# Three-layer block kernel on one core: later key blocks summed by VectorE, decays behind the last convolutions, mirror blocks of the inverse by transposes, and four moved steps

## The reference, cut to what matters

```python
proj = h @ w_in; z, xbc, dt = split(proj)             # layer 0
xbc = silu(causal_dwconv(xbc, conv_w, conv_b))        # 24 tiles of 128 channels, 4 taps
acs = cumsum(softplus(dt + dt_bias) * A)              # decays, 32 heads
y = rmsnorm_groups(ssd_scan(xs, bm, cm, acs) * silu(z)) @ w_out
modulation = silu(c) @ mod_w + mod_b                  # rows of the layers' shifts, scales and gates
```

## Time and profile before

| what | us |
|---|---|
| median of 3 runs | 2679.03 (2676.23 to 2679.85) |
| the profiled execution | 2680.78 |
| its span in the trace | 2679.0 |
| TensorE busy (13456 matmuls) | 2559.1 |
| VectorE busy | 1217.1 |
| ScalarE busy | 1061.5 |
| GpSimd busy | 972.0 |

### The profile page before, as it was taken

The page is one execution under the profiler, slowest core; times in us unless marked ns, Lnnn a source line. Parts: engine busy times, 40 slices in busy tenths (PEclk is TensorE's granted clock), DMA queues, the critical chain, the costliest instruction groups (busy, mean ns, idle before and its releaser), DMA issues.

```text
span 2679.0 us, 36867 instructions
## 1 busy us (share of the span) xinstructions
PE 2559.1 (96%) x13456; PEld 2081.0 (78%) x13456; DVE 1217.1 (45%) x2007; ACT 1061.5 (40%) x1658; POOL 972.0 (36%) x431
## 2 busy tenths in 40 slices
PE   4999989999999999999999998999899999999998
PEld 2777768877888866669888887788668888988887
DVE  6777766576545746655111127554112111531122
ACT  3466644322225246654222235713342223442232
POOL 1333334455554210013444443302214445344443
PEclk9999999999999999999999999999999999999999
DMA  6433334577653200011333331201103333133231
GB/s 256 154 107 117 103 126 142 173 234 230 215 185 121 99 24 25 17 40 60 99 99 105 94 100 58 78 10 40 55 16 95 108 112 111 63 95 101 94 110 55
DMA packets 74994, 276.55 MB, mean 103 GB/s; under 512 B 8144, under 2 KB 10576, under 8 KB 73456
## 3 DMA queue, kind: packets, MB, share of 16 engines
q1 hardware_dynamic: 56672, 201.66, 23.8%
q10 hardware_dynamic: 18192, 73.08, 7.9%
HBM read 272.54 MB, written 2.16 MB: 103 GB/s over the span
## 4 chain that ended last, share of the span: by engine, by line
PE 84%; DVE 7%; DMA 4%; issue 3%; ACT 2%; DVEq 0%; SPq 0%; POOL 0%; ACTq 0%; POOLq 0%
PE G L293 28%; PE STAT_G L293 27%; DMA mod_w<-in_modw 3%; PE B L306 2%; DVE mod_w L347 2%; PE B L580 2%; PE B L293 2%; PE B L1314 2%; PE NRM L1351 1%; PE B L2336 1%; PE B L2022 1%; DMA const<-in_const 1%; PE STAT_G L1332 1%; PE STAT_G L306 1%; PE G L306 1%
## 5 line engine op out<-in xcount | busy, mean ns | idle before, releaser
L278 POOL TENSOR_TENSOR w_lo<-raw,w_hi 128x1024 fp32r<-128x1024 f32 x375 | 933.1, 2499 | 1655.6 <-ACT w_hi L270 1650.8
L270 ACT ACTIVATE w_hi<-raw 128x1024 fp32r<-128x1024 f32 x375 | 386.7, 1052 | 311.9 <-PE STAT_G L293 127.8
L293 PE MATMUL G<-h_hi,w_hi 128*128 128x512 f32 x888 | 352.2, 397 | 1.0 <-DVE tn L978 0.8
L293 PE MATMUL STAT_G<-h_hi,w_hi 128*128 128x512 f32 x872 | 346.5, 397 | 6.4 <-POOL w_lo L278 2.0
L293 PE MATMUL G<-h_lo,w_hi 128*128 128x512 f32 x888 | 346.0, 390 | 0.0
L293 PE MATMUL G<-h_hi,w_lo 128*128 128x512 f32 x888 | 345.8, 389 | 0.0
L293 PE MATMUL STAT_G<-h_lo,w_hi 128*128 128x512 f32 x872 | 340.4, 390 | 0.0
L293 PE MATMUL STAT_G<-h_hi,w_lo 128*128 128x512 f32 x872 | 340.4, 390 | 0.0
L347 DVE SCALAR_TENSOR_TENSOR mod_w<-mod_w,const 128x1024 f32<-128x1024 f32 x96 | 189.8, 1993 | 65.4 <-DMA mod_w<-in_modw 65.3
L293 PEld LDWEIGHTS G<-h_hi,w_hi 128*128 128x128 f32 x888 | 166.9, 188 | 41.4 <-issue 7.4
L293 PEld LDWEIGHTS STAT_G<-h_hi,w_hi 128*128 128x128 f32 x872 | 164.4, 189 | 43.9 <-issue 7.1
(11 more groups left out here) (553 smaller groups left out, 4408.6 us busy)
## 6 DMA issues: line engine op xcount, KB each, us to landing
raw<-in_units SPq DMA_DIRECT2D x375, 512.0 KB, 3.6
mod_w<-in_modw ACTq DMA_DIRECT2D x96, 512.0 KB, 4.7
mod_first<-in_modw ACTq DMA_DIRECT2D x8, 1024.0 KB, 20.2
acsb<-acs ACTq DMA_DIRECT2D x16, 512.0 KB, 3.6
cw<-in_cw ACTq DMA_DIRECT2D x2, 2048.0 KB, 8.7
x<-in_x SPq DMA_DIRECT2D x1, 2048.0 KB, 26.8
out<-x SPq DMA_DIRECT2D x1, 1024.0 KB, 4.8
out<-x SPq DMA_DIRECT2D x2, 512.0 KB, 3.1
```

Of the source, the lines that this page charges most:

```text
L270: act.activation(w_hi[s][:, :], raw[s][:, :], ACT.Identity).then_inc(hi_done, 1)
L278: pool.tensor_tensor(w_lo[s][:, :], raw[s][:, :], w_hi[s][:, :].bitcast(F32), ALU.subtract).then_inc(lo_done, 1)
L293: ins = pe.matmul(out[0:m, :], a[s][:, k * P:k * P + m], b[:, c], start=(n == 0 and q == 0), stop=(n == len(blocks) - 1 and q == 2))
```

## The change

It has seven parts. (1) At the end (`post_ffn2`, no next layer) the first sums of the second half are issued in the middle of the last unit's half product. (2) At the five seams ScalarE's Ln and Exp for the second half (`late_root` of `_b`) come behind the first high part of the first half. (3) In the GDN convolutions the reciprocal and two small operations move behind convolution 6, the rest of `decays()` behind convolution 7, TensorE's turn to t = 9, VectorE's copies and the Exp to t = 10. (4) In the inverse the L1652 products go; four groups of four transposes of g_y follow each level's Y update, into the same PSUM banks, and ScalarE copies each bank to g_x. (5) In sb VectorE adds the later key blocks in pairs and threes (three adds of 128x128 per head), and TensorE does nine matmuls of 512, 384, 256 and 128 columns (triangular) and 128, 256, 128, 128 and 128 columns (-1). (6) In layer 0 the scale and scan of the decays, and the DMA of their result, move behind convolution 0. (7) The row sums move up: block 11 is loaded and summed behind convolution 7, 12 is loaded before the 16 tiles and summed before tile 8's norm, 13 before tile 12's, 14 before tile 14's, 15 behind tile 15's; ScalarE's loads of 13 to 15 stand behind output copies instead of before them.

```diff
@@ late_tensor
+                if j == 7 and not more:
+                    product_half(pe, u1 + j, hi, lo, 1, banks[1][3], range(n // 2), n)
+                    late_sums(pe, name, 1, y0, range(3))
+                    done = n // 2
                 product_half(pe, u1 + j, hi, lo, 1, banks[1][j - 4], range(done, n), n).then_inc(unit_done, 1)
...
-            late_sums(pe, name, 1, y0)
+            late_sums(pe, name, 1, y0, range(4) if more else range(3, 4))
@@ late_scalar
-            late_root(act, name + "_b", 1, h0 + POST_B, B6)
             for i in range(KC):
                 late_high(act, k0, i, 0, bcol)
+                if i == 0:
+                    late_root(act, name + "_b", 1, h0 + POST_B, B6)
@@ gdn_tensor
-                if t == 5:
+                if t == 9:
                     pe.wait_ge(gab, 9)
...
                     pe.wait_ge(inv_c, n + 1)
+                    if lv > 1:
+                        pe.wait_ge(inv_x, n - TT + 1)
                     for h in range(4):
                         ins = pe.matmul(packed(UB[c], lv, h * 64, 64), g_x[c][:, hb[h]], half(g_qs[c], lv, 1, h * P, P),
                                         start=True, stop=True)
-                    if lv < LEVELS - 1:
+                    ins.then_inc(inv_mm, 1)
+                if lv < LEVELS - 1:
+                    for c in range(TT):
+                        n = (lv - 1) * TT + c
+                        pe.wait_ge(inv_done, n + 1)
                         for h in range(4):
-                            ins = pe.matmul(packed(UB[c], lv, 256 + h * 64, 64), g_qs[c][:, hb[h]],
-                                            half(g_x[c], lv, 0, h * P, P), start=True, stop=True)
-                    ins.then_inc(inv_mm, 1)
+                            ins = pe.transpose(UB[c][:, hb[h]], g_y[c][:, hb[h]], ident)
+                        ins.then_inc(inv_t, 1)
@@ gdn_scalar
-                if t == 8:
+                if t == 10:
                     act.wait_ge(gab, 10)
...
+            for n in range((LEVELS - 2) * TT):
+                act.wait_ge(inv_t, n + 1)
+                act.activation(g_x[n % TT][:, :], UB[n % TT][:, :], ACT.Identity).then_inc(inv_x, 1)
@@ gdn_vector
-                if t == 1:
-                    decays()
                 if 4 <= t <= 11:
                     l2(t - 4)
+                if t == 6:
+                    beta()
                 if t == 7:
+                    decays()
+                if t == 10:
                     decay_columns()
@@ sb_tensor
-                        for j in range(i, 4):
-                            _, _, oj, wj = ZT[j]
-                            ins = pe.matmul(ZB[m % 2][b][:, c + (j - i) * P:c + w], cst("ntri" if i == j else "nones"),
-                                            s_sp[m % 2][:, oj:oj + wj], start=False, stop=(j == 3), skip_group_check=True)
+                        pe.matmul(ZB[m % 2][b][:, c:c + w], cst("ntri"), s_sp[m % 2][:, o:o + w], start=False,
+                                  stop=(i == 3), skip_group_check=True)
+                    pe.wait_ge(later_done, 3 * m + 3)
+                    for i, j, src in later_keys(m):
+                        b, c, o, w = ZT[i]
+                        ins = pe.matmul(ZB[m % 2][b][:, c + j * P:c + j * P + src.shape[1]], cst("nones"), src, start=False,
+                                        stop=(i == 2 or j == 2), skip_group_check=True)
@@ sb_vector
+                v.wait_ge(sp_done, n + 1)
+                v.tensor_tensor(of1, sp[:, o2 + P:o2 + 2 * P], sp[:, o3:o3 + P], ALU.add).then_inc(later_done, 1)
+                v.tensor_tensor(of0[:, 0:P], sp[:, o1 + P:o1 + 2 * P], sp[:, o2:o2 + P], ALU.add).then_inc(later_done, 1)
+                v.wait_ge(later_done, 3 * n + 2)
+                v.tensor_tensor(of0[:, P:2 * P], sp[:, o1 + 2 * P:o1 + 3 * P], of1, ALU.add).then_inc(later_done, 1)
@@ ssm_scalar
+                if t == 1:
+                    act.wait_ge(dt_v, 6)
+                    act.dma_start(dram["acs"], dts[:, 2 * T:3 * T]).then_inc(acs_out, 16)
-                if t in (2, 4):
+                if t in (2, 4, 6):
                     mod_load(act, 8 + t // 2)
...
-            mod_load(act, 11)
+            mod_load(act, 12)
...
             high(8)
-            mod_load(act, 12)
+            high(9)
             output(1)
             prep(act, u_out + 5)
-            high(9)
+            mod_load(act, 13)
...
             for o in (4, 5):
                 high(2 * o + 2)
                 high(2 * o + 3)
-                mod_load(act, 9 + o)
                 output(o)
                 prep(act, u_out + 4 + o)
+                mod_load(act, 10 + o)
             high(14)
             high(15)
-            mod_load(act, 15)
@@ ssm_vector
-            v.wait_ge(dt_v, 4)
-            v.tensor_scalar(dts[:, 0:T], dts[:, T:2 * T], nega[0:32, 1:2], None, ALU.mult).then_inc(dt_v, 1)
...
+                if t == 0:
+                    v.wait_ge(dt_v, 4)
+                    v.tensor_scalar(dts[:, 0:T], dts[:, T:2 * T], nega[0:32, 1:2], None, ALU.mult).then_inc(dt_v, 1)
+                    v.wait_ge(dt_v, 5)
+                    v.tensor_tensor_scan(dts[:, 2 * T:3 * T], const_row_ones, dts[:, 0:T], 0.0, ALU.mult,
+                                         ALU.add).then_inc(dt_v, 1)
-                if t in (1, 3, 5):
+                if t % 2:
                     mod_sum(v, 8 + t // 2)
...
-            mod_sum(v, 11)
             for o in range(4, KC):
+                if o != 5:
+                    mod_sum(v, 12 + (o - 4 if o == 4 else o - 5))
                 normal(2 * o)
                 normal(2 * o + 1)
-                mod_sum(v, 8 + o)
+            mod_sum(v, 15)
```

More of the change, by code:

```diff
@@ L539, in late_tensor, with late_sums @@
                 pre_sums(pe, name, 0, range(6, 8))
-            late_sums(pe, name, 1, y0)
-        def late_sums(pe, name, a, y0):
+            late_sums(pe, name, 1, y0, range(4) if more else range(3, 4))
+        def late_sums(pe, name, a, y0, parts=range(4)):
             p = posts[name]
@@ L547, in late_sums @@
             if a:
-                pe.wait_ge(yo_done, y0 + 6)
-                pe.matmul(out, onesf, diag[:, tokens[1]], start=True, stop=False)
-                for i in range(4):
+                if 0 in parts:
+                    pe.wait_ge(yo_done, y0 + 6)
+                    pe.matmul(out, onesf, diag[:, tokens[1]], start=True, stop=False)
+                for i in parts:
                     pe.wait_ge(ysq_done, 12 * p + 9 + i)
                     ins = pe.matmul(out, onesf, quarter(i), start=False, stop=(i == 3))
+                if 3 not in parts:
+                    return
             else:
@@ L1914, in gdn_vector @@
                     v.wait_ge(inv_mm, n + 1)
[L1915 to L1919 removed]
+                    ys = half(g_y[c], lv, 1)
+                    v.tensor_tensor(ys, ys, packed(UB[c], lv, 0, 256), ALU.subtract).then_inc(inv_done, 1)
             def values_out(c):
@@ L1975, in build, with later_sums, later_keys @@
         uS = at["sb"]
+        later_done = S("later_done")
+        def later_sums(m):
+            return sq[:, m % 2 * T:m % 2 * T + 2 * P], sq[:, m % 2 * T + 2 * P:m % 2 * T + 3 * P]
+        def later_keys(m):
+            sp, (of0, of1) = s_sp[m % 2], later_sums(m)
+            o1, o2, o3 = (ZT[i][2] for i in (1, 2, 3))
+            return ((0, 1, sp[:, o1:o1 + P]), (0, 2, of0), (1, 1, sp[:, o2:o2 + P]), (1, 2, of1), (2, 1, sp[:, o3:o3 + P]))
         def sb_tensor(pe):
@@ L2105, in sb_vector @@
                 ins.then_inc(sp_done, 1)
+                sp, (of0, of1) = s_sp[n % 2], later_sums(n)
+                o1, o2, o3 = (ZT[i][2] for i in (1, 2, 3))
+                v.wait_ge(sp_done, n + 1)
[3 more added lines that the diff above has]
+                v.tensor_tensor(of0[:, P:2 * P], sp[:, o1 + 2 * P:o1 + 3 * P], of1, ALU.add).then_inc(later_done, 1)
                 if n >= 4 and n % 2 == 0:
```

13 lines of the change are left out of this document (3 added, 10 removed).

## The result

| | before | after |
|---|---|---|
| median of the runs | 2679.44 (4 runs, 2676.23 to 2685.20) | 2639.44 (4 runs, 2633.95 to 2645.19) |
| the profiled execution | 2680.78 | 2640.55 |
| its span | 2679.0 | 2638.7 |

A forecast was written before the change was run, and what follows sets the result against it. TensorE, busy 96% of the span, was taken to bound the kernel. Terms -9.1, -5.8, -6.4, -5.1, -1.6, -1.3 and +1.2 made -28.1 from 2680.78, so 2652.7, given as 2651 with a range of 2641 to 2662.

The forecast's parts named there:

- More than the waits: Rival: output stage gains 4 more, sb 1.5, seams and start their upper bounds (3): 2643 us; chance 0.13.
- The lower clock behind that wait goes too: GDN convolutions: the half-rate stretch behind the 6.2 us wait for the Ln disappears, estimated at 1.4 us.
- sb's -5.8: sb: shorter sums save 0.91 us at five heads and 0.42 at three, adds covered: -5.8 us.
- Inverse: Inverse: transposes at 0.44 us replace 20 matmul groups at 0.893, all waits covered, full clock held: -9.1 us.
- End: Kernel's end: sums moved before the last product's end uncover VectorE's add and the Square: a loss of 1.2 us.
- The rival that the clock falls in the inverse: Rival: transposes end the full rate at each of five levels, costing 44 us more: 2695; chance 0.04.
- that a transpose costs what a matmul does: Rival, inverse: a transpose of this data is as dear as a matmul, 2660 us; chance 0.03.
- the convolutions: GDN convolutions: 6.2 us wait and 1.4 of lower clock go, 1.2 comes back: -6.4 us.
- the 1.2 of convolution 7: GDN convolutions: the moved reciprocal makes convolution 7 late, so TensorE waits 1.2 us.
- the output stage (-5.1): Layer 0's output stage: TensorE's waits of 3.7 and 1.4 us for output copies shrink to about nothing: -5.1.
- the seams (-1.3): Five seams: the wait before the first low-part product shrinks by 0.26 us each: -1.3.
- the start (-1.6): Start of layer 0: scale and scan leave the path before convolution 0, whose following product waited 1.80 us: -1.6.

The follow-up runs named there:

- e5: Parts 6 and 7 together on the kernel before: median 2666.78 against 2678.43, ratio 0.9956.
- e10: Parts 3, 4 and 5 on the kernel before: median 2658.59 against 2678.32, ratio 0.9930.
- e9: Part 2 alone on the kernel before: median 2672.95 against 2678.32, ratio 0.9980.
- e12: The kernel after with part 1 undone, timed: median 2637.15 us, where the whole change on the same chip had 2638.05.
- e11: The whole change again, unchanged: median 2638.05 against 2678.32 for the kernel before, ratio 0.9858.
- e1: The kernel before once more, unchanged: 2680.13 us.
- e4: The kernel after with part 1 undone, one execution: 2641.51 us.
- e3: Part 6 alone on the kernel before: 2678.47 us.
- e8: The kernel after without part 7, row blocks 11 to 15 loaded and summed where they were: 2641.93 us.
- e2: Part 7 alone on the kernel before: median 2669.35 against 2677.55, ratio 0.9974.
- e6: The kernel before with row sums of the reloaded buffer over 128 columns instead of 1024, loads kept: median 2670.77, ratio 0.9970.

## Why the prediction was off by its size

I go by my own steps. Taken alone the parts make -11.7 (6 and 7, e5), -19.7 (3 to 5, e10), -5.4 (2, e9) and +1.3 (1, e12), together -35.5 with an uncertainty of 3 to 5 on each of the first three, against -40.0 and -40.3 (e11) for the whole; mine made -28.1. The 4.5 between -35.5 and -40 are within these errors. My own bounds add up to -41.2, which covers the result; the range of 2641 to 2662 cut them short. In the rival *More than the waits*, the nearest to what came, seams and start at their upper bounds make 3.7 and not 3, so 2642; but it would have reached this number by waits, not by the clock.

*The step that failed: the lower clock behind waits.* The sum has it at one place only, "The lower clock behind that wait goes too ... my estimate 1.4", and puts it at nothing in the output stage, at the start and at the seams. A time can be split by the traces into work at the full clock, idle time of TensorE, and what the lower level costs, which is half of TensorE's busy time at that level. By these three my sum was -16.4, -10.3 and -1.4 (sb's -5.8 being 7.3 less work and 1.5 more waiting). The mean of before and e1 against the mean of after and e11 gives -16.2, -13.1 and -11.7. So the work was right to 0.2 (part of that is luck, since the long feed-forward stretch of before counts here as work), the waits were short by 3, and the clock by 10. What the lower level cost was 24.6 us in before, 34.5 in e1, 18.3 in after and 17.3 in e11.

*Right in mechanism and size.* Inverse: 8.85 us a level, no gap, -9.0; the 10 us that I leaned on for the clock held the transposes of rows 5 in their last 1 us only, so the full clock was settled by the runs of the change and not before. sb: -6.1, adds covered, wait of 1.8 at even heads. End: a loss of 1.28 (e4, e12) against 1.2. The rival that the clock falls in the inverse, and that a transpose costs what a matmul does, are both out.

*Right in size by luck: the convolutions.* -6.7 against my -6.4, with the 1.2 of convolution 7 where I had put it. But I had 5.0 less of waiting and 1.4 of lower clock; measured are 3.6 of waiting, since the first Ln is still 1.37 late, and 3.1 of clock. The fall behind the 6.2 held 2.88 us of busy time, so the 1.4 that I gave it is right; a second one, from 1649 to 1653, I hadn't looked for. Against the usual 145.0 us of this stretch e10 gains 7.7.

*Mis-sized: the output stage (-5.1).* "The two waits of TensorE for such copies are 3.7 and 1.4 ... -5.1" holds as far as waits go, but it is not the whole price. In six executions with the old order and whole sums (before, e1, e3, e8, e9, e10) the stretch took 118.2 to 120.3 us with 13.7 of idle time in the mean, in six with the new (after, e2, e4, e5, e11, e12) 108.7 to 110.7 with 7.5. So 6.1 are waits, against my 5.1, though not only the two I named; the lower clock cost 5.2 in the mean with the old order and 1.7 with the new, 3.5 that I had not priced. What moved in VectorE's queue are its waits for the loads: 12.7 to 17.9 us between convolution 0 and the seam with the old order, 1.6 to 3.7 with the new. This is the chain moved up one slot, which I had put at the far end of the bounds. Its row sums took 38.7 us in before and 42.4 in e1, 34.9 and 33.6 in after and e11. I had priced a sum at its duration in one row, 2.72, when it takes 1.22 alone and up to 3.4 beside a subtraction, but e2 (39.5) and e8 (36.1) show that the sums' length doesn't make the difference between the two orders.

*Mis-sized: the seams (-1.3) and the start (-1.6).* I priced the seams' wait, 0.26 each; it measured 0.25 to 0.33. Nothing behind a wait of 2 us was priced, at 1.5 for each fall. I had read the lower clock only behind the 6.2, and the profiled execution showed it behind two seams out of five, where five others of the kernels without part 2 show four or five, and e10 two. e9 puts the part at 5.4. The start gave 2.8 in the mean of all traces, 1.7 of it wait and most of the rest the fall behind it.

*The base.* "Against the profiled execution" was right for its own difference, but this execution was a light one in the convolutions (142.6 against 145.0 in five others) and at the seams, and a heavy one in the feed-forward stretch (380.7; others without part 2 374.2 to 381.3). The two nearly cancel in its total, 2680.78 against a median of 2677.92 over 35 runs. Stage by stage they don't, and a sum made of its stages took over its luck. The 6.7 us in the feed-forward stretch are mostly this luck: with part 2 it was 374.0 five times, 374.2 and 379.8 once each. Long cases (379.4 to 381.3: before, e5, e10, e4) are those in which the 72 whole sums took 146.6 us or more; in all others with whole sums it was at most 144.0. Whether the change makes the long case rarer beyond its seam is open; with whole sums it is 1 long case of 6 against 3 of 6, which doesn't settle it.

*The clock by the runs.* Each run has a mean granted clock. Over the 35 runs of before it is 0.986, over 8 of after 0.991. At half rate a share of 0.014 of 2678 us costs up to 37, a share of 0.009 of 2640 up to 23: so up to 14 of the 40 us are lower clock that no longer occurs; the traces above give 11.7. Over the 35 runs of before the time falls by 2.7 us for each 0.001 of mean clock, correlation -0.78, and over the 10 of e6 the correlation is -0.86; so this, not the row sums, is also most of the scatter that e6 kept.

*Two smaller readings of the clock.* e8 and e10 had 1.1 us less in the inverse's stretch than after because only 2.5 and 2.6 us of it, instead of 4.9, were at the lower clock, all at its start. And sb is no cheaper by clock: it ran for 13.7 us at the lower level in before and in after, and for 10.2 to 13.7 in all the others but e8 (3.4).

*What stays open.* Why a wait of 2.0 us at a seam tips the clock in 26 of 35 cases and one of 1.7 in 1 of 35 is not shown, only that it does. No run took part 2 out of the full change.

## What to carry to other kernels

When a wait in front of TensorE is shortened, look at the granted clock in the microseconds behind it, in several executions: at five seams with waits of 2.0 us it was worth some two and a half times the shortening itself, and in the output stage more than half as much as the waits. Price a stage whose queue mixes loads, sums and copies by taking the stage's whole length against its TensorE work at the full clock, and not by its longest waits. And before a sum is made of one profiled execution, compare its stretches with a second one of the same kernel; where they differ, the stretch has no single price.

## What the runs showed of the hardware that I had not expected

- A VectorE sum of 128x1024 with both inputs in SBUF takes 1.22 us alone and 3.40 beside GpSimd's subtraction; one of 128x128 0.29 and up to 2.55. In the feed-forward stretch the same 72 sums took 138.6 us in after and 151.7 in before, though in each about half of them met a subtraction.
- The lower clock behind a wait: at the seams behind 26 of 35 waits of 2.0 us and behind 1 of 35 of 1.7, with the same work on both sides; it began 0 to 1.5 us behind the first matmul. At the start of layer 0 it came behind a wait of 1.8 in six executions of six.
- Transposes through TensorE, 0.44 us for four of 128x128, one fifth of the time for 32 us on end, left the granted clock at 1.00.
- One unchanged kernel runs the same stretch in 375.7 or 380.7 us.
